# One-column side steps spread over the long section, and an earlier fetch of the first projection's weights, in a two-network transformer kernel

## What is computed

```python
for l in range(2):                                   # first network
    sh1, sc1, g1, sh2, sc2, g2 = modulation(c, w_mod[l], b_mod[l])        # silu(c) @ w_mod[l] + b_mod[l]
    csh1, csc1, cg1, csh2, csc2, cg2 = modulation(c_ctx, w_mod[l], b_mod[l])
    hx = modulate(rms_norm(x, norm1_g[l]), sh1, sc1)     # 512 tokens
    hc = modulate(rms_norm(xc, norm1_g[l]), csh1, csc1)  # 256 context tokens
    px = hx @ w_in[l]                                    # "first projection", 1024 -> 1696
    ...                                                  # attention, Fourier and Hyena mixers
    x = x + g1 * heads_out(att_x, px, hy, w_out[l])
    x = x + g2 * sq_relu_mlp(modulate(rms_norm(x, norm2_g[l]), sh2, sc2), w_mlp1[l], w_mlp2[l])
    ...                                                  # the same for xc in layer 0
...
for layer in range(2):                               # second network
    mod = cond @ ada_w[layer] + ada_b[layer]         # 1024 x 6144, one condition vector
    ...
```

## Time and profile before

| | |
|---|---|
| median of 3 runs | 3961.41 us (3959.11 to 3965.34) |
| profiled execution | 3957.06 us, of which the span is 3955.3 us |
| PE busy | 3573.3 us (90%), 17828 instructions |
| PE weight loads | 2893.0 us (73%) |
| DVE busy | 1941.0 us (49%), 2682 instructions |
| ACT busy | 1329.7 us (34%), 1800 instructions |
| mean granted PE clock | 0.947 of full speed |
| DMA | 360.63 MB, 91 GB/s in the mean |

### The profile page before, as it was taken

The page is one execution under the profiler, slowest core; times in us unless marked ns, Lnnn a source line. Parts: engine busy times, 40 slices in busy tenths (PEclk is TensorE's granted clock), DMA queues, the critical chain, the costliest instruction groups (busy, mean ns, idle before and its releaser), DMA issues. The chain is left out here.

```text
span 3955.3 us, 42614 instructions
## 1 busy us (share of the span) xinstructions
PE 3573.3 (90%) x17828; PEld 2893.0 (73%) x17828; DVE 1941.0 (49%) x2682; ACT 1329.7 (34%) x1800; POOL 5.2 (0%) x12
## 2 busy tenths in 40 slices
PE   7899988999789999789995998799969999978998
PEld 3685557888678755588883777788858888767887
DVE  5436447777543444455544555433344545544333
ACT  3322343331213423353334444422343323343223
POOL 0000000000000000000000000000000000000000
PEclk9899998999899999999997999899979999989999
DMA  4331013445541130135531221122223333212221
GB/s 168 132 117 44 11 38 112 144 149 174 172 128 64 54 101 1 43 130 174 186 107 47 64 64 65 64 96 96 81 54 80 80 77 74 81 54 75 96 96 54
DMA packets 366621, 360.63 MB, mean 91 GB/s; under 512 B 65071, under 2 KB 312030, under 8 KB 365023
## 3 DMA queue, kind: packets, MB, share of 16 engines
q1 hardware_dynamic: 366211, 357.84, 29.5%
q10 hardware_dynamic: 220, 0.07, 0.0%
HBM read 350.02 MB, written 4.72 MB: 90 GB/s over the span
## 5 line engine op out<-in xcount | busy, mean ns | idle before, releaser
L385 PE MATMUL ps<-second_h_hi,second_w_hi 128*128 128x512 f32 (+1 forms) x1776 | 685.8, 386 | 75.6 <-DVE second_h_lo L608 46.9
L385 PE MATMUL ps<-second_h_lo,second_w_hi 128*128 128x512 f32 (+1 forms) x1776 | 667.6, 376 | 0.0
L385 PE MATMUL ps<-second_h_hi,second_w_lo 128*128 128x512 f32 (+1 forms) x1776 | 667.1, 376 | 0.0
L457 DVE TENSOR_TENSOR second_w_lo<-ring,second_w_hi 128x2048 fp32r<-128x2048 f32 (+2 forms) x140 | 290.8, 2078 | 440.0 <-ACT second_w_hi L409 440.0
L385 PE MATMUL ps<-h_mix_hi,w_hi 128*128 128x512 f32 (+1 forms) x1192 | 425.3, 357 | 50.9 <-DVE h_mix_lo L608 25.5
L385 PEld LDWEIGHTS ps<-second_h_hi,second_w_hi 128*128 128x128 f32 x1776 | 348.6, 196 | 136.4 <-issue 54.3
L385 PE MATMUL ps<-h_mix_lo,w_hi 128*128 128x512 f32 (+1 forms) x1192 | 419.4, 352 | 0.0
L385 PE MATMUL ps<-h_mix_hi,w_lo 128*128 128x512 f32 (+1 forms) x1192 | 418.4, 351 | 0.0
L385 PEld LDWEIGHTS ps<-second_h_hi,second_w_lo 128*128 128x128 f32 x1776 | 346.9, 195 | 58.0
L385 PEld LDWEIGHTS ps<-second_h_lo,second_w_hi 128*128 128x128 f32 x1776 | 348.4, 196 | 55.9 <-issue 1.7
L409 ACT ACTIVATE second_w_hi<-ring 128x2048 fp32r<-128x2048 f32 (+2 forms) x140 | 243.5, 1740 | 237.5 <-PE ps L385 227.7
(11 more groups left out here) (369 smaller groups left out, 5310.4 us busy)
## 6 DMA issues: line engine op xcount, KB each, us to landing
ring<-in_w_mlp SPq DMA_DIRECT2D x64, 1024.0 KB, 5.4
side_w<-in_ada_w SPq DMA_DIRECT2D x96, 512.0 KB, 4.7
ring<-in_ffn_w_in SPq DMA_DIRECT2D x44, 1024.0 KB, 5.1
side_w<-in_w_mod SPq DMA_DIRECT2D x80, 512.0 KB, 3.8
ring<-in_attn_w_in SPq DMA_DIRECT2D x48, 512.0 KB, 5.3
ring<-in_hgrn_w_in SPq DMA_DIRECT2D x32, 512.0 KB, 5.4
ring<-in_ffn_w_out SPq DMA_DIRECT2D x16, 1024.0 KB, 5.1
ring<-in_w_in SPq DMA_DIRECT2D x14, 1024.0 KB, 5.3
```

The source lines that it names most:

```text
L385: mm = pe.matmul(acc, lhsT, rhs, start=k == 0 and wp == ap, stop=k == j.kt - 1 and wp == 1)
L457: dve.tensor_tensor(unit.place(unit.slot[1]), unit.place(M.ring[:, u % RING, :]), unit.place(unit.slot[0]), ALU.subtract).then_inc(*S.w_lo ...
```

## The change

```diff
@@ SideThread @@
-    def __init__(self, R, plan, sw, sa, start, pitch, gains, lag=2):
+    def __init__(self, R, plan, sw, sa, start, pitch, gains, lag=2, free=()):
...
-            self.times.append(self.times[-1] + pitch * side.n)
+            self.times.append(self.times[-1] + pitch[side.n - 1])
...
             yield self.times[0] - 1 if i < 2 else self.at(former, 2 * r + 2)
+            if i == 0:
+                for sig, value in self.free:
+                    sp.wait_ge(sig.sem, sig.at(value))
@@ @@
-SIDE_PITCH = 2.35
+SIDE_PITCH = 6.4, 4.7
@@ first_layer, first section @@
-                           (len(R.jobs) - 4) / (2 * len(SIDES_IN)), {})
+                           (0, (len(R.jobs) - 4) / len(SIDES_IN)), {})
@@ first_layer, long section, last layer @@
-            pitch = ((n_up - 0.3) * 8 * jobs_a_unit - 2 * len(outer) * n_late) / 12
+            pitch = ((n_up - 0.3) * 8 * jobs_a_unit - 2 * len(outer) * n_late) / 12,
@@ opening @@
-            AheadThread(X, [px_cut(io, 0, c) for c in (512, 256)], 100, (S["tokens_summed"], T // P)),
+            AheadThread(X, [px_cut(io, 0, c) for c in (512, 256)], 60, (S["tokens_summed"], T // P)),
```

More of the change, by code:

```diff
@@ L731 @@
     WIDE = 512
-    def __init__(self, R, plan, sw, sa, start, pitch, gains, lag=2):
+    def __init__(self, R, plan, sw, sa, start, pitch, gains, lag=2, free=()):
         self.S, self.M, self.plan, self.sw, self.sa = R.S, R.M, plan, sw, sa
-        self.gains, self.lag = gains, lag
+        self.gains, self.lag, self.free = gains, lag, free
         self.times, self.done = [start], [0]
         for side, _ in plan:
-            self.times.append(self.times[-1] + pitch * side.n)
+            self.times.append(self.times[-1] + pitch[side.n - 1])
             self.done.append(self.done[-1] + (KD - 1) * side.n)
```

## The result

| | before | changed |
|---|---|---|
| median of the runs made side by side | 3963.28 us (3959.11 to 3965.34, 4 runs) | 3903.53 us (3903.09 to 3905.21, 4 runs) |
| profiled execution | 3957.06 us, span 3955.3 us | 3903.11 us, span 3901.3 us |
| mean granted PE clock | 0.947 | 0.954 |

The changed kernel takes 0.9851 of the time of before, 95% interval 0.9834 to 0.9868: faster, by 59.8 us between the medians and by 54.0 us between the two profiled spans. The forecast was 3912 us, a gain of 49.2 us.

A forecast was written before the change was run, and what follows sets the result against it. PE, busy 90% of the span, was taken to lose time to late one-column side fetches; -47.9 + 2.4 - 3.7 = -49.2 us against the median of 3961.41 us gave 3912 us, with an 8-in-10 range of 3902 to 3928 us.

The forecast's parts named there:

- The one-column units: Long section, 957 to 1150 us: all the time lost to late side-weight fetches comes back, -47.9 us.
- The sign that I had named: Behind the first one-column fetch: no side-sum wait above 1 us for 160 us, and a clock of 1.00.
- The page's fit: Side fetches: 3.2 us for 512 KB, so they would keep up and the long section would win nothing.
- The norm: End of the long section: side steps now stand in DVE's chain and make PE late, +2.4 us.
- The last units beside the projection: Jobs 144 to 152, beside 512-column jobs and a DVE that mostly waits: no cost.
- The opening: Before the first job matmul: earlier ring fetches let it start sooner, at about 142.4 us, -3.7 us.
- The last weight fetches behind side fetches: Projection, rival: ring fetches wait behind side fetches, 24.5 us for seven units, 3936 us; chance 0.10.
- the slower case: MLP and projection, rival: some 19 ring fetches from job 75 on stand behind side fetches, 4015 us; chance 0.03.
- The fetches were never the brake: One-column stretch, rival: something else slows it and stays, only opening and norm count, 3960 us; chance 0.03.

The follow-up runs named there:

- two banks and two buffers: Changed kernel at the old pitch of 2.35 jobs, sums of odd one-column units in a PSUM bank of their own: 3930.26 us, ratio 0.9923.
- the run with narrow fetches: Changed kernel at the old pitch of 2.35, one-column units fetching only 64 of 512 weight columns, all steps kept: 3928.04 us, ratio 0.9928.
- pitch 4.7: Changed kernel with 4.7 jobs for a one-column unit instead of 6.4: 3905.71 us, ratio 0.9862.
- the two kernels with two banks and prompt fetches: Changed kernel at pitch 2.35, second PSUM bank for odd one-column units' sums, with 64-column fetches (3904.42 us) or a third weight buffer (3904.14 us).
- pitch 5.2: Changed kernel with 5.2 jobs for a one-column unit instead of 6.4: 3911.04 us, ratio 0.9873.
- the side steps alone: Changed kernel with only the new pitch, the fetch of the first projection's weights left at 100 as before: 3911.04 us, ratio 0.9875.
- three (one bank): Changed kernel at the old pitch of 2.35, whole fetches, a third weight buffer for one-column units: 3929.84 us, ratio 0.9932.
- pitch 3.3: Changed kernel with 3.3 jobs for a one-column unit instead of 6.4: 3905.62 us, ratio 0.987.

## Why the prediction was right, and where its reason was not whole

**The one-column units, -47.9 us.** Measured: 50.7 us less in the part of the section, of which 2.8 us only moved behind the first norm sum, so 47.9 us. The way of sizing it held: the loss was read as the time of the stretch less its work at the undisturbed rate, and the change gave back all of it. That way does not depend on the cause. The sign that I had named came too: no wait of a side sum in that stretch, and a clock of 1.00.

**The cause was half of the cause.** I wrote that the fetches are late because of two buffers, 2.85 us a fetch at least and 3.65 us in practice, against 2.67 us that the jobs leave, "so PE has to wait for them". The gap between 2.85 and 3.65 us should have made me look further. The earlier trace rows named the other half: PE waited for `mods`, the store of the *former* unit, and not for the accumulator of its own. I read this as a consequence of late fetches. With the fetches out of the way 24 us stayed; with the store out of the way 26.6 us; with both, nothing. The wider pitch removes both, as it leaves 6.4 jobs for a unit's fetches and puts more than five jobs between a store and the next sum. Curing the late fetches alone gave back 23.6 and 24.0 us, half of what I had put down to them. That the edit removes the other brake too, which the forecast did not know, was luck. One thing stays open. By the formula, late fetches alone cost (2.85 - 2.67) x 48 = 8.6 us, and with two banks and two buffers 26.6 us were lost, at 3.36 us a fetch; what holds a fetch between 2.85 and 3.36 us there was not taken apart.

**The page's fit.** By the estimate of 3.2 us from the fit of the Trainium skill's page "DMA: Bandwidth & Descriptors", section "Anatomy of one DMA — SWDGE (gpsimd) path", a fit for another issuing path, the change would have won nothing in the long section. The landings of 512 KB measured here (3.7 to 5.0 us in the medians of stretches) are all above it. And the run with narrow fetches shows that fetches that keep up would not have freed the stretch either: this rival was built on my cause, and fell with it.

**The norm, +2.4 us.** Measured +2.2 us, shown by the interval of 29.72 us against 27.50, and by its return to 27.48 us where the last unit ends sooner. PE's wait for the 512 tokens' `h_mix_lo` went from 1.88 to 3.48 us and that for the context's from 1.69 to 2.29 us, while that of its norm sum for `rs` fell from 2.05 to 1.27 us: not all of it at the place that I named. In the section it costs less than 2.2 us: with the last unit ended sooner (pitch 4.7, and the two kernels with two banks and prompt fetches) the section is 777.9 to 778.0 us against 779.2 and 779.5, and of the 2.2 us, 0.95 us are the side sum that moved into the norm and would else be done ahead of it.

**The last units beside the projection, nothing.** Right for the change: the last part grew by 2.0 us, which are its two sums. At pitch 5.2 the end of the last unit fell beside the 256-column jobs and cost 3.7 us there in the one trace taken, a kind of place that my sum did not price and that 6.4 passes without a loss.

**The opening, -3.7 us.** In the two profiled executions -3.6 us, first matmul at 142.46 us where about 142.4 was given, ring fetches at 105.43 us where about 104.5 was. Over all eleven traces with this edit the first matmul starts between 139.5 and 144.1 us, and at 146.1 and 146.7 in the two without. Between medians, though, the edit is worth 6.0 us (alone, 11 runs against 15) and 7.2 us (the changed kernel against the side steps alone). The term had the chain in the opening right and left out the first projection behind it, which had its shorter form in eight of eleven traces with the edit and in neither of the two without. Whether the edit brings that about is open (last section).

**The rivals.** The last weight fetches behind side fetches, and the slower case in the same place, did not come: PE waited 1.9 us for `w_lo` in the whole long section, as it had before. *The fetches were never the brake* was half true as to its reason and wrong as to its number, since the other brake went by the same edit.

**The rest.** Forecast 3912, measured 3903.5 us. The sum of terms, -49.2 us, stands against -50.0 us in the two places that the edits touch (-46.4 - 3.6). Another 4 us of the 54.0 us between the spans lie in sections that were not changed (first projection -2.9, second mixers -1.3). And 3.9 us come from what I added: I put the median 4.35 us above the profiled execution, as it was for the kernel before, while the changed kernel's median lies 0.4 us above its own. Together, 0.8 + 4.0 + 3.9 us are the distance between forecast and result.

## What to carry to other kernels

Size a loss as the stretch's time less its work at the rate of an undisturbed stretch; here it gave 47.9 us, and 47.9 us came back, though the cause was only half understood. Then read the releaser of each wait word by word: waiting for the *former* unit's store is another thing than waiting for this unit's input, and a formula that gives 2.85 us where 3.65 us are measured leaves room for a second cause. A store of 0.15 us that is queued behind seven steps of later units can stop PE although DVE is busy for only 94.6 of 168 us; a second place for the result cures that, more buffers cure late fetches, and spreading the work in time cures both.

## What the runs showed of the hardware that was not expected

**Landing times.** The same 512 KB fetch landed in 3.7 us in the median at 141 GB/s in the stretch (the change), in 4.2 us at 185 GB/s (before) and in 5.0 us at 210 GB/s with up to three in flight; the 64 KB fetch took 2.0 us. It is not the traffic alone: at the same 197 GB/s it took 4.1 us with two buffers (two banks) and 5.0 and 4.5 us, by the buffer that it went to, with three (one bank). A third buffer made each fetch slower and bought little throughput, as two buffers reached 197 GB/s, and 202 GB/s at pitch 3.3 with 4.3 us to landing.

**Sections that do not repeat.** The first projection took 127.9 to 128.0 us in eight traces and 130.8 to 131.1 us in five, with the same instructions in it. Windows of 20 us, PE alone, of the changed kernel and of the kernel with pitch 4.7, from 180 us:

```profile
180.00:200.00 20.00, 19.61 (x122) 1.00 0.42 132
...
240.00:260.00 20.00, 20.00 (x114) 1.00 0.24 76
```
```profile
180.00:200.00 20.00, 19.61 (x108) 0.91 0.40 132
...
240.00:260.00 20.00, 19.64 (x108) 0.91 0.26 79
```

The wait in the first window is the same (19.61 us busy in both), and the granted clock is 1.00 in the one and 0.91 in the other, with 14 matmuls fewer. The second mixers took between 248.0 and 254.3 us likewise, and all that follows them between 2303.5 and 2309.2 us. Whether the opening's edit makes the shorter form of the first projection more likely stays open: both traces without it had the longer one, and three of the eleven with it.
